# Two feed-forward networks in split fp32: down projections by Strassen's scheme for 8 of 22 feature tiles per group

## The reference, cut to what matters

```python
def swiglu(h, w_gate_up, w_down):
    gu = jnp.einsum('bsd,df->bsf', h, w_gate_up)
    gate, up = jnp.split(gu, [FFN_HIDDEN], axis=-1)
    return jnp.einsum('bsf,fd->bsd', jax.nn.silu(gate) * up, w_down)
...
    f = (jax.nn.gelu(g, approximate=True) * u) @ w_down[l]
    h = h + _rmsnorm(f, post_ffn_gain[l])
```

## Time and profile before

| what | value |
|---|---|
| median of 3 runs | 2669.07 us (2668.92 to 2669.63) |
| span of the profiled execution, first to last instruction | 2666.9 us |
| its own time outside the span | not recorded; the median lies 2.2 us above the span |
| TensorE busy | 2653.3 us, 99% |
| VectorE busy | 1686.8 us, 63% |
| ScalarE busy | 1252.5 us, 47% |
| GpSimd busy | 3.5 us |
| moved from HBM | 493.93 MB, 186 GB/s |
| four down stages on TensorE | 1408 matmuls on line 2057 and 704 on line 2063 |

### The profile page before, as it was taken

One profiled execution on the slowest core, in us unless ns is written; L12 is line 12 of the kernel. 1 busy time (PEld: TensorE's weight loads), 2 busy tenths in 40 slices (PEclk: granted clock), 3 DMA queues, 4 the chain that ended last, 5 costly groups with the idle time before them and its releaser, 6 DMA issues.

```text
span 2666.9 us, 37509 instructions
## 1 busy us (share of the span) xinstructions
PE 2653.3 (99%) x14046; PEld 2292.2 (86%) x14046; DVE 1686.8 (63%) x1769; ACT 1252.5 (47%) x1285; POOL 3.5 (0%) x8
## 2 busy tenths in 40 slices
PE   9999999999999999999999999999999999999998
PEld 8888888888888888888888888888888888888887
DVE  7646666665555555545555568888777764577755
ACT  6544444444445444334444456645554444444443
POOL 0000000000000000000000000000000000000000
PEclk9999999999999999999999999999999999999999
DMA  6554555455555555555555555543555555555554
GB/s 250 190 189 174 174 188 189 168 194 189 214 196 175 189 188 204 189 200 188 189 188 188 189 185 176 168 155 133 205 174 189 189 207 191 185 189 189 189 193 138
DMA packets 73021, 497.22 MB, mean 186 GB/s; under 512 B 8311, under 2 KB 9560, under 8 KB 14824
## 3 DMA queue, kind: packets, MB, share of 16 engines
q1 hardware_dynamic: 72936, 496.06, 53.6%
HBM read 493.93 MB, written 2.10 MB: 186 GB/s over the span
## 4 chain that ended last, share of the span: by engine, by line
PE 97%; DVE 1%; DMA 1%; ACT 1%; SPq 0%; issue 0%; DVEq 0%; ACTq 0%
PE acc L2001 38%; PE acc L2009 20%; PE acc L2057 16%; PE acc L2063 8%; PE acc L2142 7%; PE acc L2147 3%; PE acc L2269 1%; PE acc L2031 1%; DMA mask_s<-in_mask 1%; PE aux L2410 1%; PE aux L2351 0%; PE aux L2174 0%; PE aux L2182 0%; PE acc L2038 0%; PE acc L2276 0%
## 5 line engine op out<-in xcount | busy, mean ns | idle before, releaser
L1158 DVE TENSOR_TENSOR w_lo<-raw,w_hi 128x2048 fp32r<-128x2048 f32 (+1 forms) x467 | 1047.9, 2244 | 525.0 <-ACT w_hi L644 457.4
L644 ACT ACTIVATE w_hi<-raw 128x2048 fp32r<-128x2048 f32 (+1 forms) x467 | 876.0, 1877 | 878.8 <-PE acc L2001 348.5
L2001 PE MATMUL acc<-xa,w_hi 128*128 128x512 f32 x4480 | 1071.4, 391 | 0.0
L2001 PEld LDWEIGHTS acc<-xa,w_hi 128*128 128x128 f32 x4480 | 824.7, 188 | 161.0 <-issue 0.7
L2009 PEld LDWEIGHTS acc<-xa,w_lo 128*128 128x128 f32 x4480 | 574.4, 191 | 21.7
L2009 PE MATMUL acc<-xa,w_lo 128*128 128x256 f32 x4480 | 581.5, 283 | 0.0
L2057 PE MATMUL acc<-w_hi,hid 128*128 128x512 f32 x1408 | 335.5, 390 | 0.0
L2057 PEld LDWEIGHTS acc<-w_hi,hid 128*128 128x128 f32 x1408 | 263.9, 188 | 54.4
L1170 DVE TENSOR_TENSOR tmp<-acc,small 128x512 f32<-128x512 f32 x120 | 83.0, 692 | 263.3 <-ACT small L654 262.9
L2142 PE MATMUL acc<-w_hi,xa 128*128 128x512 f32 x768 | 182.4, 390 | 0.0
L2063 PE MATMUL acc<-w_lo,hid 128*128 128x512 f32 x704 | 175.5, 389 | 0.0
(11 more groups left out here) (347 smaller groups left out, 1480.8 us busy)
## 6 DMA issues: line engine op xcount, KB each, us to landing
raw<-in_w_in SPq DMA_DIRECT2D x158, 1024.0 KB, 4.9
raw<-in_w_gate_up SPq DMA_DIRECT2D x88, 1024.0 KB, 4.9
raw<-in_w_up SPq DMA_DIRECT2D x87, 1024.0 KB, 4.9
raw<-in_w_down SPq DMA_DIRECT2D x80, 1024.0 KB, 4.9
raw<-in_w_out SPq DMA_DIRECT2D x32, 1024.0 KB, 4.9
raw<-in_w_down SPq DMA_DIRECT2D x16, 512.0 KB, 3.6
raw<-in_w_uq SPq DMA_DIRECT2D x3, 1024.0 KB, 4.9
h_tok<-in_x_tok SPq DMA_DIRECT2D x1, 2048.0 KB, 9.2
```

What stands on the lines that cost most here:

```text
L644: act.activation(hi_part(u, run)[:, 0:kt * P], raw[:, u % RAW, 0:kt * P], ACT.Copy).then_inc(hi_made, splits(u, run))
L1158: dve.tensor_tensor(lo_part(u, run)[:, 0:kt * P], raw[:, u % RAW, 0:kt * P], hi_part(u, run)[:, 0:kt * P], ALU.subtract).then_inc(lo_made, ...
L2001: last = pe.matmul(acc[:, bnk], w_hi[:, u % SPLIT, k * P:(k + 1) * P], x[:, k0 + k], start=first and k == 0, stop=False)
```

## The change

A down stage of a group becomes two passes of two columns each. Within a pass the 22 feature tiles go two ways. Tiles 0 to 7 form a 2 x 2 block matrix against the two columns: activations by two token blocks and two sets of four tiles, weights by two sets of four tiles and two columns. Its product takes seven block products (`M_1` to `M_7`) for eight, in Winograd's form of Strassen's scheme, each of 12 matmuls. Tiles 8 to 19 stay plain, three units of 24 matmuls for each column (`PLAIN_1` to `PLAIN_6`), and tiles 20 and 21 of both columns share one unit (`MIXED`). That is 14 units (`FORMS`) and 11 loads (`PIECES`) for a pass.

Four of the products need differences of weight blocks. GpSimd makes them in fp32 (`weight_sum`), two into the new buffer `w_sum` and two in place in a slot of `raw`; ScalarE and VectorE split them like any unit. Block pieces stay in their slot until the last difference that reads them. The activations' sums are made once per group from `hid` by VectorE (`hidden_sums`) ahead of the last two rounds of `gated`, which are taken out of the loop for that, and split by ScalarE (`sums_high`) and VectorE (`hidden_low`). `x_sums` and `w_sum` are the same memory, so the first difference of a group waits for `x_sums_lo`.

The scheme adds products that several outputs share. It is done by snapshots: a bank goes on accumulating, and at four points of a pass (`snap`, after `M_1`, `M_5`, `M_6`, `M_7`) its state is added to `h_tok`, or copied or added to `ff_out`. TensorE waits for a snapshot before it goes on in that bank. `snap` and `h_add` are VectorE's, with one operand in PSUM; only in the first group of the second network ScalarE does the snapshots, and VectorE, in ScalarE's place, reads the columns' ends. Squares, transposes and gains of finished columns move to other units. Some semaphores of the mixers are merged (their waits are the same), and two buffers (`last_row`, `ff_end`) move, so that `last_row` is loaded later. The diff, cut to its core (the second network's loops are changed in the same way):

```diff
...
-DOWN = 6
-FF_UNITS = 2 * GT + COLS * DOWN
+FORMS = 14
+PASSES = COLS // 2
+FF_UNITS = 2 * GT + PASSES * FORMS
...
+PLAIN_1, M_1, M_5, M_2, PLAIN_2, M_6, M_3, M_7, PLAIN_3, M_4, MIXED, PLAIN_4, PLAIN_5, PLAIN_6 = range(FORMS)
+PIECES = (
+    (0, ((8, 0), (9, 0), (10, 0), (11, 0))),
+    (1, ((0, 0), (1, 0), (2, 0), (3, 0))),
+    (2, ((4, 1), (5, 1), (6, 1), (7, 1))),
+    (3, ((0, 1), (1, 1), (2, 1), (3, 1))),
+    (0, ((4, 0), (5, 0), (6, 0), (7, 0))),
+    (1, ((12, 0), (13, 0), (14, 0), (15, 0))),
+    (1, ((16, 0), (17, 0), (18, 0), (19, 0))),
+    (2, ((20, 0), (21, 0), (20, 1), (21, 1))),
+    (3, ((8, 1), (9, 1), (10, 1), (11, 1))),
+    (1, ((12, 1), (13, 1), (14, 1), (15, 1))),
+    (0, ((16, 1), (17, 1), (18, 1), (19, 1))),
+)
+B_11, B_22, B_12, B_21 = 1, 2, 3, 4
+PIECE_OF = {PLAIN_1: 0, M_1: B_11, M_2: B_21, M_3: B_22, PLAIN_2: 5, PLAIN_3: 6, MIXED: 7, PLAIN_4: 8, PLAIN_5: 9, PLAIN_6: 10,
+            M_7: B_12, M_4: B_21}
+FREED_BY = (None, None, None, None, PLAIN_1, M_1, PLAIN_2, M_3, M_7, PLAIN_3, M_4)
...
+            def down_loads(u, src):
+                for n in range(len(PIECES)):
+                    slot = PIECE_RAW[u, n][0]
+                    if n < 4:
+                        sp.wait_ge(lo_made, u + n - 3)
+                    else:
+                        sp.wait_ge(lo_made, u + FREED_BY[n] + 1)
+                    if n == 5:
+                        sp.wait_ge(w_summed, sums_before(u) + 1)
+                    if n == 7:
+                        sp.wait_ge(w_summed, sums_before(u) + 3)
+                    sp.dma_start(raw[:, slot], src[n]).then_inc(raw_loaded[slot], 16)
...
+            def sums_high(n):
+                act.wait_ge(x_summed, 5 * (n + 1))
+                act.activation(s_14_hi[:], x_sums[:, 4:8], ACT.Copy).then_inc(x_sums_hi, 1)
+                act.activation(s_2_hi[:], x_sums[:, 0:4, 0:P], ACT.Copy).then_inc(x_sums_hi, 1)
+                act.activation(hid[:, 0:4, P:S], x_sums[:, 0:4, P:S], ACT.Copy).then_inc(x_sums_hi, 1)
...
+            def weight_sum(u, n):
+                if n == 1:
+                    pool.wait_ge(x_sums_lo, 3 * (sums_before(u) // 8 + 1))
+                    if sums_before(u):
+                        pool.wait_ge(lo_made, PASS_STARTS[sums_before(u) // 4 - 1] + M_6 + 1)
+                    piece_loaded(u, B_11)
+                    piece_loaded(u, B_12)
+                    out_, a, b = w_sum[:], piece(u, B_12), piece(u, B_11)
+                if n == 2:
+                    pool.wait_ge(lo_made, u + M_5 + 1)
+                    piece_loaded(u, B_22)
+                    out_, a, b = w_sum[:], piece(u, B_22), w_sum[:]
+                if n == 3:
+                    pool.wait_ge(w_summed, sums_before(u) + 2)
+                    out_, a, b = piece(u, B_12), piece(u, B_22), piece(u, B_12)
+                if n == 4:
+                    pool.wait_ge(lo_made, u + M_2 + 1)
+                    pool.wait_ge(w_summed, sums_before(u) + 2)
+                    out_, a, b = piece(u, B_21), piece(u, B_21), w_sum[:]
+                pool.tensor_tensor(out_, a, b, ALU.subtract).then_inc(w_summed, 1)
...
+            def hidden_sums(n, ready):
+                dve.wait_ge(op_hi, ready)
+                dve.wait_ge(op_lo, ready)
+                dve.tensor_tensor(x_sums[:], hid[:, 0:8, 0:S], hid[:, 0:8, S:2 * S], ALU.add).then_inc(x_summed, 1)
+                x_11, x_21, x_12, x_22 = x_sums[:, 0:4, 0:P], x_sums[:, 0:4, P:S], x_sums[:, 4:8, 0:P], x_sums[:, 4:8, P:S]
+                for m, (out_, a, b, op) in enumerate(((x_22, x_21, x_22, ALU.add), (x_21, x_11, x_21, ALU.subtract),
+                                                      (x_11, x_22, x_11, ALU.subtract), (x_12, x_12, x_11, ALU.subtract))):
+                    dve.wait_ge(x_summed, 5 * n + m + 1)
+                    dve.tensor_tensor(out_, a, b, op).then_inc(x_summed, 1)
+            def hidden_low(n):
+                for m, (out_, x, high_) in enumerate(((s_14_lo[:], x_sums[:, 4:8], s_14_hi[:]),
+                                                      (s_2_lo[:], x_sums[:, 0:4, 0:P], s_2_hi[:]),
+                                                      (hid[:, 0:4, S + P:2 * S], x_sums[:, 0:4, P:S], hid[:, 0:4, P:S]))):
+                    dve.wait_ge(x_sums_hi, 3 * n + m + 1)
+                    dve.tensor_tensor(out_, x, high_, ALU.subtract).then_inc(x_sums_lo, 1)
+            def snap(u, bnk, form, out_):
+                dve.wait_ge(lo_used, u + form + 1)
+                dve.tensor_tensor(out_, out_, acc[:, bnk], ALU.add).then_inc(snapped, 1)
...
-                for n in range(COLS):
-                    for j in range(DOWN):
-                        if j == DOWN - 1:
-                            dve.wait_ge(lo_used, u1 + DOWN * (n + 1))
-                            h_add(n, t1 + 2 * n)
-                        split(u1 + DOWN * n + j + 2)
-                        if j == DOWN - 1:
-                            dve.wait_ge(h_added, 2 * COLS * (g + 1) + 2 * n + 2)
-                            dve.sem_inc(acc_free, 2)
-                        if g and n and j == 2:
-                            tokens_low(n - 1, DT, V_LAT, gain)
-                        if g and n and j == 3:
-                            final_gain(n - 1)
+                def added(n, u, form):
+                    dve.wait_ge(lo_used, u + form + 1)
+                    dve.wait_ge(snapped, 8 * g + 4 * (n // 2) + 4)
+                    h_add(n, t1 + 2 * n)
+                    dve.wait_ge(h_added, 2 * COLS * (g + 1) + 2 * n + 2)
+                    dve.sem_inc(acc_free, 2)
+                for p in range(PASSES):
+                    u, t = u1 + FORMS * p, t1 + 4 * p
+                    b_11, b_21, b_12, b_22 = (bank(t + n) for n in range(4))
+                    for form in range(FORMS):
+                        if form == M_6:
+                            snap(u, b_22, M_6, h_tok[:, 2 * p + 1, 0])
+                        if form == M_7:
+                            snap(u, b_22, M_7, h_tok[:, 2 * p, 1])
+                        if form == MIXED:
+                            added(2 * p, u, MIXED)
+                        if form == PLAIN_6:
+                            added(2 * p + 1, u, PLAIN_6)
+                        split(u + form + 2)
+                        if form == M_5:
+                            snap(u, b_22, M_1, h_tok[:, 2 * p, 0])
+                            snap(u, b_12, M_5, h_tok[:, 2 * p + 1, 1])
+                        if g and p and form == PLAIN_3:
+                            tokens_low(1, DT, V_LAT, gain)
+                        if g and p and form == M_4:
+                            final_gain(1)
+                        if g and form == PLAIN_6:
+                            tokens_low(2 * p, DT, V_LAT, gain)
+                            final_gain(2 * p)
...
+            def product(u, t, x_hi, x_lo, first=False, final=False, more=False):
+                pe.wait_ge(hi_made, u + 1)
+                for k in range(4):
+                    w = w_hi[:, u % SPLIT, k * 512:(k + 1) * 512]
+                    pe.matmul(acc[:, bank(t)], x_hi(k), w, start=(first and k == 0), stop=False,
+                              skip_group_check=more)
+                    last = pe.matmul(acc[:, bank(t)], x_lo(k), w, start=False, stop=False, skip_group_check=more)
+                last.then_inc(hi_used, 1)
+                pe.wait_ge(lo_made, u + 1)
+                for k in range(4):
+                    last = pe.matmul(acc[:, bank(t)], x_hi(k), w_lo[:, u % SPLIT, k * 512:(k + 1) * 512],
+                                     start=False, stop=(final and k == 3), skip_group_check=more)
+                last.then_inc(lo_used, 1)
...
+                pe.wait_ge(acc_free, b_21 + 1)
+                plain(PLAIN_1, b_11, 8, first=True)
+                pe.wait_ge(acc_free, b_22 + 1)
+                product(u + M_1, b_22, *hidden(0, 0), first=True, final=True)
+                pe.wait_ge(x_sums_lo, 3 * (group + 1))
+                product(u + M_5, b_12, *sums_14(1), first=True, final=True)
+                product(u + M_2, b_11, *hidden(4, 0))
+                plain(PLAIN_2, b_11, 12)
+                pe.wait_ge(snapped, snaps + 1)
+                product(u + M_6, b_22, *SUMS_2, final=True, more=True)
+                pe.wait_ge(snapped, snaps + 2)
+                product(u + M_3, b_12, *sums_14(0), more=True)
+                pe.wait_ge(snapped, snaps + 3)
+                product(u + M_7, b_22, *hidden(0, 1), final=True, more=True)
+                plain(PLAIN_3, b_11, 16)
+                product(u + M_4, b_21, *hidden(4, 1))
+                if p == 0:
+                    pe.wait_ge(op_lo, v1 + GT)
+                pe.wait_ge(snapped, snaps + 4)
+                both_columns(u + MIXED, t)
+                plain(PLAIN_4, b_12, 8)
+                if not staggered:
+                    plain(PLAIN_5, b_12, 12)
+                    plain(PLAIN_6, b_12, 16, final=True)
...
```

(67 more changed lines are left out.)

309 lines of the change are left out of this document (199 added, 110 removed).

## The result

The changed kernel takes **2744.79 us** (median of 4 runs, 2738.23 to 2747.11), the kernel before beside it 2669.35: a ratio of 1.0279, 95% interval [1.0266, 1.0292], 75.4 us slower. The forecast was 59.7 slower, 2729, with a range of 2664 to 2790. The profiled execution took 2743.8 us, its span is 2742.0, 75.1 above the span of before.

A forecast was written before the change was run, and what follows sets the result against it. TensorE's matmuls, plus holes opened where GpSimd's sums hold VectorE's subtractions, bound the kernel. Stalls of 81.5 us less 21.8 us of saved matmuls give +59.7 on 2669.1: 2729 us, bounds 2708 to 2790, stated range 2664 to 2790.

The forecast's parts named there:

- the forecast's own case: Down stages: GpSimd's weight sums hold VectorE's subtractions, so TensorE waits; 59.7 us slower, 2729, chance 0.78.
- the 81.5 booked: Stalls of TensorE summed over the eight down passes, from 6.4 us in a settled pass to 14.0: 81.5 us.
- The bounds: Other sum durations, other orders of waiting and transfers never overlapping put the time between 2708 and 2790 us.
- 96 fewer matmuls, 21.8 us: Down passes take 252 matmuls instead of 264, saving 2.72 us in each of 8 passes if nothing waits.
- rival 1: No holding of VectorE's subtractions by GpSimd: only late copies for M_5 remain, 9 us; 2656 us, chance 0.10.
- The hold: A GpSimd sum and a VectorE weight subtraction, both reading SBUF, wait for each other; up to 4.3 us per sum.
- Rivals 1 and 2: Rival 2: partial holding of VectorE, two thirds of the stalls vanish, 2665 to 2700 us, chance 0.07.
- A sum's duration, taken as 4.3: One GpSimd weight difference of 128x2048 floats takes 4.3 us, with bounds of 4.16 and 5.13.
- near the slope: GpSimd sum time extrapolated from 128x512 (1.28 us) and 128x256 (0.80 us): 4.16 by slope, 5.13 by proportion.
- Settled pass: A down pass that isn't a group's first: TensorE waits before M_2, PLAIN_2 and M_6, 6.4 us in all.
- rival 3: Clock drops to 1.2 GHz in TensorE's holes, half-speed products after some 14: 38 us more, 2767 to 2800; chance 0.05.
- What would show it: TensorE busy near 2632 us, holes before M_2, PLAIN_2 and M_6, subtractions up to 6.5 us, sums of 4.2 to 5.1.

The follow-up runs named there:

- experiment 1: The changed kernel without its 32 weight differences, GpSimd only clearing w_sum and one column (four products multiply wrong weights): 2660.8 us, 0.9972.
- Experiment 7: The changed kernel without weight differences, and the first FFN's last-pass token tiles of a pass's first column prepared one unit earlier: 2653.99 us, 0.9947.
- experiment 2: The changed kernel with each weight difference replaced by two GpSimd clearings of the same tile, which write but read nothing: 2664.6 us.
- experiment 5: The changed kernel with all four weight differences of a pass made on VectorE instead of GpSimd: 2668.3 us, 0.9999.
- experiment 10: The kernel before plus 16 useless GpSimd sums, each between two tiles, in the first FFN alone: 2671.61 us, 1.0013.
- experiment 3: The changed kernel with each weight difference done as four GpSimd instructions of 512 columns: 2724.18 us, 1.021.

## Why the prediction was right, point by point

- **Direction, mechanism and range: right.** The time is in the forecast's own case. It was 15.7 us too low; 8.2 of that are in the down stages (89.7 against 81.5) and 7.2 outside. That the stages come so close is in part luck. TensorE's 32 waits there make its matmuls start 64.8 us late in all (59.1 us of it idle), 16.7 less than the 81.5 booked, and 17.1 us of matmuls at half clock and 7.8 us of wider spacing behind the holes, for which nothing was booked, more than make up for it.
- **The bounds: added up wrongly.** By its own terms (77 us of stalls and 10 off; 104, 11 and 15 on) they are 2714 and 2777, not 2708 and 2790. The measured time lies inside both.
- **96 fewer matmuls, 21.8 us: right** as TensorE's work; experiments 1 and 7 show it less the late copies of M_5, which rival 1 had put at 9 us.
- **The hold: right**, and settled by experiments 2, 5 and 10. "I let the later comer wait in either direction and serve them in order of arrival" is what the rows after show. The Trainium skill (SBUF — State Buffer, Who interferes with whom) has a GpSimd instruction that only writes not contending; experiment 2 agrees, with 2.29 us beside a clearing. Rivals 1 and 2 fall: a subtraction beside a running sum ends 2.15 us behind the sum's end, so nothing of it is done meanwhile, neither all (rival 1) nor a part (rival 2). It keeps its 2.29 us only where nothing is read.
- **A sum's duration, taken as 4.3: wrong, 4.60 to 4.66 where a sum runs alone.** It was inside the bounds of 4.16 and 5.13. The step that failed is "near the slope": the two rows' slope was too flat. By the prediction's own values (87 us at 4.50, 104 at 5.13) 4.63 would have given some 90 us of stalls. The Trainium skill (GPSIMD Engine Reference, Performance versus the Vector engine) has 4.50, nearer than mine and 3% under the trace.
- **The holes one by one.** Settled pass: 1.8, 1.85, 2.75 expected ahead of M_2, PLAIN_2, M_6; 2.18, 0.15, 2.66 us of idle time measured in the first FFN, 2.18, 1.79, 2.70 and 2.18, none, 2.66 in the second. First pass of the first FFN: M_5 0.39 + 0.21 (1.65 + 0.45 expected), PLAIN_2 1.22 (1.35), M_6 2.69 (2.75), M_3 3.56 (3.65), PLAIN_1 none (1.85). M_6 came as booked in all eight passes (2.66 to 2.70). M_3 did in three of the five passes that have a hole there and measured 1.97 and 1.09 in the others, and PLAIN_2 is 0.2 or nothing in three passes. By pass, idle time is 8.1, 5.0, 8.0, 6.4, 9.2, 6.7, 11.1 and 4.8 us, 59.1 in all, against 11.8, 6.4, 11.8, 10.7, 14.0, 6.4, 14.0 and 6.4. The beginning of a group's first pass was booked too dear above all: M_1 in the second FFN measured 1.73 and 1.86 for 3.95.
- **The clock (rival 3, 0.05): partly true at the same time as the forecast.** 17.1 us of the stages' 89.7 are at half clock, 7 us of which, in three stages, were shown to be a net loss. The earlier trace rows bore on it: 0.61 over the 9 us behind the last matmul is some 2 us at 2.4 GHz and 7 at 1.2 GHz, so the clock fell there after some 2 us without a matmul, less than several of the forecast holes. It should have been a term of the sum, with a size of 7 to 17, and not a rival of 38.
- **Outside the stages, booked at nothing: 7.2 us.** The working costed the token squares and copies inside the last pass, but not that a column pair finishes later than one column did, so its token tiles come late for the next projection. Experiment 7 gets 3.8 of it back by one unit's shift. The rest, 3.4 us in the mixer and the second FFN, was not taken apart.
- **What would show it.** TensorE busy was forecast near 2632 and is 2664.6: half-clock matmuls and refills after holes count as busy; without sums it is 2637.1. Subtractions up to 6.5: 6.70.

The large gain of experiment 5 I did not foresee. The prediction treated VectorE as the late engine, and it was late only by waiting.

## What to carry to other kernels

Work moved to an idle engine is not free because that engine is idle: ask whether it holds the engine whose results are awaited, and count the two in turns, in both directions. The same hold cost 2.9 us for 16 sums beside units of 5.44 us (experiment 10) and 84 us for 32 where products follow each other by 2.72 us and wait for the sums (experiment 1); cutting it in pieces moved the delay to whoever waits for the sum (experiment 3). Where holes open in a dense matmul stream, add a term for matmuls at half clock behind some of them.
